# A hybrid decoder step on one core: where small loads, the convolution, the output weights and one projected block stand in the order

## The reference

```
h = RMSNorm(x);  p = h @ w_in                      # 1024 -> 2816 columns
group A (8 heads x 64): token shift  xs = p + (p_prev - p) * mu, LoRA decay, rate and gate,
    generalized delta-rule scan over tokens, GroupNorm per head, bonus, gate
group B (512 channels): u = value * sigmoid(gate); causal depthwise convolution, width 31;
    LayerNorm per token; z = z * sigmoid(z)
x = x + concat(yA, yB) @ w_out                     # group B is the lower half of w_out's rows
x = x + MoE(RMSNorm(x))                            # top 4 of 32 experts, clamped SwiGLU, d_ff 1024
y = RMSNorm(x)
```

## Time and profile before

| what | value |
|---|---|
| device time, median of 3 runs | 1236.3 us (1232.82 to 1236.37) |
| the profiled execution | 1236.51 us, its span 1234.7 us |
| mean granted TensorE clock | 0.993 of full speed |
| TensorE busy | 1192.9 us (97%), 8039 matmul records |
| VectorE busy | 452.5 us (37%) |
| ScalarE busy | 194.5 us (16%) |
| GpSimd busy | 73.5 us (6%) |
| read from HBM | 424.93 MB, mean 348 GB/s with the writes |
| instruction blocks fetched (queue q8) | 43 packets, 0.70 MB |

### The profile page before, as it was taken

How to read it: one execution, slowest core, us unless ns; L and a number is a source line. 1 busy time by engine, 2 the same in 40 slices (tenths; PEclk the granted TensorE clock), 3 DMA queues, 4 the chain that set the end, 5 groups by cost and what they waited for, 6 DMA issues and landing times.

```text
span 1234.7 us, 19155 instructions
## 1 busy us (share of the span) xinstructions
PE 1192.9 (97%) x8039; PEld 541.2 (44%) x8039; DVE 452.5 (37%) x987; ACT 194.5 (16%) x387; POOL 73.5 (6%) x113
## 2 busy tenths in 40 slices
PE   7999998999999999999999999999999999999995
PEld 5667798854333333333333333333333333333332
DVE  6657754243522333322222223323222222222324
ACT  3362223224100001100100000011000010000102
POOL 0303443030000000000000000000000000000000
PEclk9999999999999999999999999999999999999998
DMA  9521003288999999999999999999999999999994
GB/s 267 168 69 47 10 12 131 83 302 299 412 424 427 427 429 427 429 427 429 428 428 428 429 428 428 429 428 430 427 430 428 428 428 428 428 429 428 428 428 156
DMA packets 54637, 430.26 MB, mean 348 GB/s; under 512 B 13215, under 2 KB 26959, under 8 KB 29742
## 3 DMA queue, kind: packets, MB, share of 16 engines
q1 hardware_dynamic: 53146, 429.30, 84.1%
q10 hardware_dynamic: 1436, 0.16, 0.1%
HBM read 424.93 MB, written 4.48 MB: 348 GB/s over the span
## 4 chain that ended last, share of the span: by engine, by line
PE 66%; DMA 19%; DVE 2%; issue 0%; POOL 0%; ACT 0%; DVEq 0%
PE bank L1802 40%; DMA ring<-in_w_up_dram 19%; PE bank L1780 6%; PE bank L1856 5%; PE bank L1787 2%; PE bank L1027 2%; PE bank L1112 2%; PE bank L1670 2%; PE bank L1731 1%; PE bank L1810 1%; PE bank L983 1%; PE bank L1008 1%; PE bank L1828 1%; PE bank L1165 0%; PE bank L1161 0%
## 5 line engine op out<-in xcount | busy, mean ns | idle before, releaser
L1802 PE MATMUL bank<-ring,arena 128*64 128x512 f32 x1536 | 342.2, 594 | 7.2 <-DMA ring<-in_w_up_dram 6.5
L1802 PE MATMUL bank<-arena 128*64 128x512 f32 x1536 | 342.6, 593 | 6.5 <-DMA arena<-in_w_up_dram 6.5
L1802 PEld LDWEIGHTS bank<-ring,arena 128*64 128x64 f32 x1536 | 109.2, 137 | 218.5 <-issue 200.5
L1802 PEld LDWEIGHTS bank<-arena 128*64 128x64 f32 x1536 | 108.9, 136 | 217.5 <-issue 199.4
L2074 DVE TENSOR_SCALAR arena<-bank 128x512 f32<-128x512 f32 x32 | 22.1, 692 | 380.4 <-PE bank L1810 380.4
L2088 DVE TENSOR_TENSOR arena<-arena,bank 128x512 f32<-128x512 f32 x186 | 113.7, 679 | 1.6 <-PE bank L1856 1.6
L524 PE MATMUL bank<-arena,ring 128*128 128x336 f32 x352 | 104.0, 453 | 1.2 <-DVE arena L660 1.2
L1856 PE MATMUL bank<-arena 64*128 64x512 f32 (+1 forms) x384 | 91.1, 606 | 0.7 <-issue 0.7
L1780 PE MATMUL bank<-arena 128*64 128x512 f32 (+1 forms) x384 | 89.5, 600 | 0.1
L2078 DVE TENSOR_SCALAR arena<-bank 128x512 f32<-128x512 f32 x32 | 22.1, 691 | 176.6 <-PE bank L1810 176.6
L524 PEld LDWEIGHTS bank<-arena,ring 128*128 128x128 f32 x352 | 67.3, 193 | 35.0 <-issue 3.5
(11 more groups left out here) (356 smaller groups left out, 824.2 us busy)
## 6 DMA issues: line engine op xcount, KB each, us to landing
ring<-in_w_gate_dram SPq DMA_DIRECT2D x32, 2048.0 KB, 24.8
arena<-in_w_up_dram SPq DMA_DIRECT2D x32, 2048.0 KB, 27.9
ring<-in_w_down_dram SPq DMA_DIRECT2D x32, 2048.0 KB, 31.3
arena<-in_w_gate_dram SPq DMA_DIRECT2D x32, 2048.0 KB, 26.5
ring<-in_w_up_dram SPq DMA_DIRECT2D x32, 2048.0 KB, 29.0
arena<-in_w_down_dram SPq DMA_DIRECT2D x31, 2048.0 KB, 30.9
ring<-in_w_in_dram SPq DMA_DIRECT2D x11, 1024.0 KB, 5.3
ring<-in_w_out_dram SPq DMA_DIRECT2D x4, 1024.0 KB, 9.2
```

The lines of the kernel that those rows point to most:

```text
L1802: mm = M.matmul(bank[64 * hb:64 * hb + 64, b, :], tokens(cc), w[:, c, 512 * hb:512 * hb + 512], start=(cc == 0), stop=(w3 == 2 and cc == K ...
```

## The change

- **Start.** The second tile of x (128 rows) is loaded from ScalarE's queue instead of SyncE's, and ScalarE also takes its sum of squares; VectorE keeps the other two. One VectorE operation, 384 wide, makes the three diagonal tiles. The three products with ones go to PSUM bank 7, side by side, VectorE reads them there for `hT`, and the ScalarE copies and the buffer `rbc` are gone. `keep(7)` comes first among ScalarE's copies of x, since bank 7 has to be free. Six, four and three products of ones with ones (`idle_product`), whose result nobody reads, stand at the start of TensorE's list, ahead of the products with 1/rms, and behind them.
- **Vector loads.** Six of ScalarE's vector loads and the convolution weights and shift state move behind its copies of x. `project(1)` stands ahead of the transposes that use them.
- **Order of columns.** `IN_ORDER` takes the second half of the convolution's columns (units 8 and 10) ahead of the keys (2 and 3). `lay_out(2)` and `lay_out(3)` move up with them. TensorE's small products keep their order but stand behind other projections: `project(12)` ahead of `cumulate(2)`, three projections ahead of the key squares' sums, and all projections ahead of the bonus sums. ScalarE takes the exponentials ahead of the key squares.
- **Convolution.** All 124 steps are in stage one; `CONV_LATE`, `conv_late` and the waits for it in stage two are gone. VectorE runs 69 steps in a row after the second shift.
- **Output weights.** Each of the four `w_out` units is issued at a milestone of its own of the scan (`sk_done` 2, `n_done` 2, `e_ready` 3, `e_ready` 9).
- **Gates of z.** ScalarE's first sigmoid stands before the chunk loop, the other three in its first three passes; VectorE multiplies each in the same pass.
- **Projected blocks.** `project_z(0)` stands in the last pass of the chunk loop, ahead of its products; the third stage has blocks 1 to 7, in PSUM banks exchanged by one, and what stood after block d now stands after block d + 1. The four products and four additions that finish y are interleaved, and TensorE's first block of y waits for them one by one.

```diff
-CONV_LATE = 11
...
-IN_ORDER = [7, 9, 6, 2, 3, 8, 10, 0, 1, 4, 5]
+IN_ORDER = [7, 9, 6, 8, 10, 2, 3, 0, 1, 4, 5]
...
-rbc = take(NT)
...
-        sp.dma_start(xt[:, 1, :], a["x_prompt"][0, P - META:2 * P - META, :]).then_inc(x_in[1], 16)
...
+        act.dma_start(xt[:, 1, :], a["x_prompt"][0, P - META:2 * P - META, :]).then_inc(x_in[1], 16)
...
+        def load_vectors(first, last):
+            for k in range(first, last):
+                name, n = vectors[k]
...
+                act.dma_start(vrow[at:at + n, 0, :], src.rearrange("(c p) -> c p", p=P))\
+                    .then_inc(R["rows_in"], 16)
+
+        load_vectors(0, 7)
+        act.wait_ge(R["small_set"], 1)
+        act.wait_ge(x_in[1], 16)
+        A.activation(junk[1], xt[:, 1, :], ACT.Square, accum_out=small[:, 9:10]).then_inc(R["sq_ready"], 1)
+        act.wait_ge(R["ms_ready"], 1)
+        A.activation(small[:, 4:7], small[:, 0:3], ACT.Sqrt).then_inc(R["rms_ready"], 1)
+
+        def keep(c):
+            A.copy(xkeep[c], bank[:, c, 0:NT]).then_inc(R["xkeep_ready"], 1)
+
+        act.wait_ge(R["x_turned"], 3)
+        keep(KC - 1)
+        for c in range(KC - 1):
+            if c == 6:
+                act.wait_ge(R["idle_done"], 1)
+            keep(c)
+        load_vectors(7, len(vectors))
         act.dma_start(vrow[0:CW * 4, 1, :],
                       a["dw_weight"][0].rearrange("t (c p) -> (t c) p", p=P)).then_inc(R["rows_in"], 16)
         act.dma_start(vrow[0:NSEQ * NBA, 2, :],
                       a["state_shift"][0].rearrange("s (c p) -> (s c) p", p=P)).then_inc(R["rows_in"], 16)
-        act.wait_ge(R["ms_ready"], 1)
-        A.activation(small[:, 4:7], small[:, 0:3], ACT.Sqrt).then_inc(R["rms_ready"], 1)
-
-        def keep(c):
-            A.copy(xkeep[c], bank[:, c, 0:NT]).then_inc(R["xkeep_ready"], 1)
-
...
+        evacuate(6)
...
-        evacuate(6)
         evacuate(7)
...
         evacuate(8)
+        lay_out(2)
         for j in range(4):
...
         evacuate(9)
+        lay_out(3)
         for j in range(4):
...
         evacuate(10)
+        act.wait_ge(R["xkeep_stored"], 32)
+
+        def exps(j):
+            act.wait_ge(R["cum_done"], j + 1)
+            lx, li = bank[:, 4 + 2 * (j % 2), 0:NT], bank[:, 5 + 2 * (j % 2), 0:NT]
+            A.activation(eLx[:, j, :], lx, ACT.Exp)
+            A.activation(emL[:, j, :], li, ACT.Exp, scale=-1.0)
+            A.activation(eL[:, j, :], li, ACT.Exp).then_inc(R["exp_ready"], 1)
+
+        exps(0)
+        exps(1)
+        evacuate(11)
+        exps(2)
+        exps(3)
+        evacuate(12)
+        evacuate(13)
         act.wait_ge(R["shifted"], k_last)
         for j in range(4):
             A.activation(sqT[:, j, :], kT[:, j, :], ACT.Square, scale=vecA[:, V_KK + j:V_KK + j + 1])
...
-
...
-        evacuate(12)
-        lay_out(2)
-        evacuate(13)
-        lay_out(3)
+        evacuate(14)
...
-        evacuate(14)
+        evacuate(15)
...
-        for n in range(15, 20):
+        for n in range(16, 22):
             evacuate(n)
...
-        evacuate(20)
-        evacuate(21)
...
+        def idle_product(n):
+
+            for _ in range(n):
+                mm = M.matmul(bank[:, 6, 384:512], ones, ones, start=True, stop=True)
+            return mm
+
+        idle_product(6)
         for i, (t0, n) in enumerate(TILES):
             pe.wait_ge(x_in[i], 32 if i != 1 else 16)
             for c in range(KC):
                 mm = M.transpose(bank[:, c, t0:t0 + n], xt[0:n, i, P * c:P * c + P], ident[0:n, 0:n])
             mm.then_inc(R["x_turned"], 1)
+        idle_product(4)
         pe.wait_ge(R["rdiag_ready"], 1)
+        pe.wait_ge(R["xkeep_ready"], 1)
         for i, (t0, n) in enumerate(TILES):
-            M.matmul(bank[:, 5 + i, 384:384 + n], ones[0:n, :], rdiag[0:n, i, 0:n], start=True, stop=True)\
-                .then_inc(R["rbc_done"], 1)
+            mm = M.matmul(bank[:, 7, t0:t0 + n], ones[0:n, :], rdiag[0:n, i, 0:n], start=True, stop=True)
+        mm.then_inc(R["rbc_done"], 1)
+        pe.wait_ge(R["xkeep_ready"], 2)
+        idle_product(3).then_inc(R["idle_done"], 1)
...
-                pe.wait_ge(R["xkeep_ready"], n + 1)
+                pe.wait_ge(R["xkeep_ready"], n + 2)
...
         project(0)
+        project(1)
         pe.wait_ge(R["rows_in"], 16 * 15)
...
-        for n in range(1, 8):
+        for n in range(2, 8):
...
         project(11)
+        project(12)
         pe.wait_ge(R["exp_ready"], 1)
         cumulate(2)
         pe.wait_ge(R["exp_ready"], 2)
         cumulate(3)
-        project(12)
-        project(13)
+        for n in range(13, 16):
+            project(n)
         pe.wait_ge(R["exp_ready"], 3)
         pe.wait_ge(R["kk_sq"], 4)
...
-        project(15)
+        project(16)
+        project(17)
         pe.wait_ge(R["knx_ready"], 1)
...
-        for n in range(16, 20):
+        for n in range(18, 22):
             project(n)
...
-        project(20)
-        project(21)
...
-            dve.wait_ge(x_in[i], 32 if i != 1 else 16)
+            if i == 1:
+                continue
+            dve.wait_ge(x_in[i], 32)
             last = V.tensor_tensor_reduce(out=junk[i][0:n, :], in0=xt[0:n, i, :], in1=xt[0:n, i, :], scale=1.0,
...
+        dve.wait_ge(R["sq_ready"], 1)
...
-        for i in range(3):
-            last = V.tensor_scalar(rdiag[:, i, :], ident, small[:, 12 + i:13 + i], None, ALU.mult)
-        last.then_inc(R["rdiag_ready"], 1)
+        V.tensor_tensor(rdiag, b2(ident, 3), b3(small[:, 12:15], P), ALU.mult).then_inc(R["rdiag_ready"], 1)
         dve.wait_ge(R["g_in"], 16)
-        dve.wait_ge(R["x_turned"], 3)
-        dve.wait_ge(R["rbc_ready"], 3)
+        dve.wait_ge(R["rbc_done"], 1)
         for c in range(KC):
-            dve.wait_ge(R["xkeep_ready"], c + 1)
-            V.scalar_tensor_tensor(hT[:, c, :], xkeep[c], gcol[:, c:c + 1], rbc, ALU.mult, ALU.mult)\
-                .then_inc(R["hT_ready"], 1)
+            dve.wait_ge(R["xkeep_ready"], c + 2 if c < KC - 1 else 1)
+            V.scalar_tensor_tensor(hT[:, c, :], bank[:, 7, 0:NT], gcol[:, c:c + 1], xkeep[c],
+                                   ALU.mult, ALU.mult).then_inc(R["hT_ready"], 1)

...
-        for i, n in enumerate((6, 7, 7, 7, 7, 7)):
-            convolve(n)
+        convolve(6)
+        shift(0)
+        convolve(7)
+        shift(1)
+        convolve(69)
+        for i in range(2, 6):
             shift(i)
-        convolve(21)
+            convolve(10 if i < 5 else 6)
         dve.wait_ge(R["kk_sq"], 4)
         dve.wait_ge(R["ktmp_ready"], 4)
         dve.wait_ge(R["shifted"], 6)
         link(V.tensor_tensor(kT, kT, ktmp, ALU.mult))
-        dve.wait_ge(R["exp_ready"], 4)
-        link(V.tensor_tensor(kT, kT, emL, ALU.mult))
-        convolve(2)
         dve.wait_ge(R["kk_root"], 1)
         link(V.tensor_scalar(knorm, knorm, 1e-12, None, ALU.max))
         V.reciprocal(knorm, knorm).then_inc(R["kk_inv"], 1)
-        convolve(8)
+        dve.wait_ge(R["exp_ready"], 4)
+        link(V.tensor_tensor(kT, kT, emL, ALU.mult))
         shift(6)
-        convolve(6)
+        convolve(2)
         shift(7)
...
-        shift(8)
         link(V.tensor_tensor(bT, bT, emL, ALU.mult))
-        convolve(3)
+        convolve(2)
         shift(9)
...
-        for i, n in enumerate((5, 8, 8, 8)):
-            convolve(n)
-            shift(10 + i)
-        convolve(4 * CW - CONV_LATE - 113)
+        for i in range(10, 14):
+            shift(i)
...
-    sp.wait_ge(S["conv_step"], CONV_LATE)
-    for t in range(UNITS_IN, UPRE):
+    for t, (s, n) in zip(range(UNITS_IN, UPRE), (("sk_done", 2), ("n_done", 2), ("e_ready", 3), ("e_ready", 9))):
+        sp.wait_ge(S[s], n)
         load_unit(sp, t)
...
-    pool.wait_ge(S["conv_step"], CONV_LATE)
...
+
+    def z_gate(j):
+        act.wait_ge(S["z_affine"], j + 1)
+        nc.scalar.activation(zsg[:, j, :], zT[:, j, :], ACT.Sigmoid).then_inc(S["z_sig"], 1)
+
+    z_gate(0)
...
-        if c < 4:
-            act.wait_ge(S["z_affine"], c + 1)
-            nc.scalar.activation(zsg[:, c, :], zT[:, c, :], ACT.Sigmoid).then_inc(S["z_sig"], 1)
+        if c < 3:
+            z_gate(c + 1)
...
+        else:
+            project_z(pe, 0)
...
-        for _ in range((0, 6, 5, 0)[l]):
-            next(conv)
...
-        if c:
-            dve.wait_ge(S["z_sig"], c)
-            V.tensor_tensor(zT[:, c - 1, :], zT[:, c - 1, :], zsg[:, c - 1, :], ALU.mult)\
+        if c < 4:
+            dve.wait_ge(S["z_sig"], c + 1)
+            V.tensor_tensor(zT[:, c, :], zT[:, c, :], zsg[:, c, :], ALU.mult)\
                 .then_inc(S["zT_ready"], 1)
...
+def project_z(pe, d):
+
+    if d == 0:
+        pe.wait_ge(S["zT_ready"], 4)
+        wait_unit(pe, UNITS_IN)
+        wait_unit(pe, UNITS_IN + 1)
+    if d >= 2:
+        pe.wait_ge(F["zp_ready"], d - 1)
+    for cc in range(4, 8):
+        mm = nc.tensor.matmul(bank[:, (d + 1) % 2, 0:NT], out_rows(cc)[:, P * d:P * d + P], zT[:, cc - 4, :],
```

(25 more changed lines are left out.)

102 lines of the change are left out of this document (30 added, 72 removed).

## The result

The changed kernel takes 1242.4 us (median of 9 runs, 1236.7 to 1245.9) against 1236.4 for the kernel before in the same comparison: ratio 1.0042, 95% interval 1.0026 to 1.0057. It is slower by about 6 us, where 11 us less was forecast. The profiled execution took 1245.88 us with a span of 1244.1, 9.4 more than the one of before; among the 9 runs it is the slowest, so its sum is 3 us too large for the median.

The account below looks back on a forecast made before the run. TensorE was taken as the bound up to the experts, then the full DMA weight stream. Terms summed to -11.1 us, taking 1236.5 to 1225.4, say 1225.5, with a range of 1221.5 to 1233.

Parts of the forecast that it names:

- The stream: Experts: weight loads run without a hole from the ninth, so time saved earlier passes one for one; 11 us.
- first rival: Stage one: GpSimd's product waits 9 us during VectorE's 69 steps, gate products 6 late; price 7; 22% with milder cases.
- the race: Stage one: TensorE's key sums against VectorE's sixth shift and ScalarE's key squares; +0.5 us, bounds 0 and +4.5.
- Rows of x: Start: x on two queues and quicker 1/rms rows bring the first projection earlier; -1.8 us, bounds -0.5 and -4.
- shorter path: Start: VectorE reads the 1/rms products from PSUM itself, 1.4 us in place of 2.76; -1.35 us.
- Idle products: Start: they keep TensorE working, so its clock rises before the first projection; -2.2 us, at worst 0.
- Late vectors: Start: small vector loads moved behind the copies of x may land late; +0.5 us, bounds 0 and +4.
- Order of columns: Stage one: TensorE's wait of 1.82 us for exponentials goes, -1.8 us; the race comes in its place.
- Hole: Stage two: TensorE's 2.29 us hole after four loads issued at once goes when they are spaced; -2.3, at worst 0.
- Clock: Low-clock stretches go: behind the stage-two hole, -1.6 us, and at the z block in the last chunk, -3.0 us.
- Gate ahead of the loop: Before the chunk loop: a table load and pass on ScalarE precede the first negated U; +0.5 us, at worst +1.8.
- Less cover: After the chunk loop: each later step has one projected block less ahead of it; +0.7 us, bounds 0 and +2.3.

Follow-up runs that it names:

- e11_mended: Changed kernel with x on SyncE's queue, two small loads earlier, two VectorE pauses, eleven steps fewer before sixth shift, first z gate behind first U: 1230.7 us.
- e1_pause: Changed kernel with two pauses in VectorE's run of 69 steps, waiting for GpSimd's third and fourth products: 1238.6 us.
- e3_one_queue: Changed kernel with the second tile of x back on SyncE's queue: 1240.4 us.
- e7: Kernel before with the changed start, idle products included, and x all on SyncE's queue: 1233.2 us.
- e10: Kernel before with the changed start and x all on SyncE's queue, but without the idle products: 1237.0 us.
- e5_spaced_alone: Kernel before with one edit, the last three output weight units issued behind separate level steps instead of at once: 1236.5 us.
- e6_block_alone: Kernel before with first projected block in the last chunk pass, first gate ahead of the loop, gates multiplied in the same pass, last mean rows singly: 1236.7 us.
- e12_gate_ahead: e11_mended with the first gate of z ahead of the chunk loop, as in the change: 1231.3 us.
- e9_gate_behind: Changed kernel with the first gate of z back behind the first negated U: 1240.7 us.

## Why the prediction was wrong

**The stream.** Right: 9.3 us at the ninth load, 9.4 in the span, and -3.7 and -4.1 for the mended version.

**The step that failed** is the choice between the forecast and the first rival, "shut out". The sum took VectorE's run at 0.476 us a step with 2.6 us in all for sharing with GpSimd, and put GpSimd's delay at nothing, with the median of 14 subtractions as evidence. In its place the product took 10.14 us, and TensorE lost 6.0 us waiting and 3.1 at the lower clock. The rival's mechanism, place and wait came out as written (gate products 6 us late; measured 6.01), and its price was 7; the pauses of e1_pause gave 3.8 back in the medians, and the race behind them took 3.3. What misled me was a median of another operation. The instructions of the product's own line in the kernel before:

```profile
L318 POOL TENSOR_TENSOR arena<-arena x4: 892/896/897, 31.7 to 96.5; 128x336 f32<-128x336 f32 x4
```

All four ran while VectorE did nothing, so no row had the product beside convolution steps. Of the 14 subtractions ten met steps, and nine of these were over in 0.64 to 1.5 us, beside runs of 3 to 8 steps; the tenth, 4.67, ended 0.5 us after its run of eight. That row, and not the median, was the one like the new code. Why GpSimd gets in at some places and at others not, these runs leave open. It isn't the 69 steps alone: in the changed kernel two subtractions later on took 3.39 and 2.50 us beside runs of 18 and 10 steps, and each ended 0.5 us after its run. The Trainium skill (SBUF — State Buffer, SBUF: two separate sides) says that a VectorE instruction with two SBUF inputs and a GpSimd instruction that reads SBUF exclude each other, and that whoever comes first has the ports for the whole instruction. By it GpSimd would wait for one step. The trace agrees that one keeps the other out and differs in the length: back to back, 20 steps pass (10.14 us); with a short gap between steps, none (0.94).

**Rows of x.** Predicted -1.8, with bounds -0.5 and -4; measured +0.63 at the first projection. The step "the second queue could bring rows earlier" looked at the tile that came earlier and not at the one that shares the engines with it. On one queue the first projection is at 13.51 in e3_one_queue, -0.35, but at up to 14.95 in other profiles. Of the 1.35 for the shorter path, 1.04 are seen there (1.72 us from the products with ones to the first projection, before 2.76), but these products start 0.69 later than at 11.10, behind ScalarE's second table load, which I had not counted.

**Idle products.** -2.2; the first two projections take 2.2 less than before, and 1.7 less than without these products (e7 and e10). Right, and the time shows 3.8 in the medians.

**Late vectors.** +0.5; the wait is 0.91. Right within bounds.

**Order of columns.** The wait of 1.82 for exponentials is gone, as forecast. The race, +0.5 with a bound of +4.5, measured 3.3 in e1_pause and nothing with eleven steps fewer ahead of the shift. The bound does not come out of its own terms: 99 steps at 0.53 give 70.7 against 67.6, so +3.1, and the measured wait lies just above it. (In the same way, all bounds at their good ends give 1221 only with the early rows of x in it, and 1223 without.)

**Hole.** -2.3 against -1.9 in the changed kernel's chain: right there, and by luck. The cause as I put it, a queue four loads deep, fell with e5_spaced_alone. The mean product's wait went from 1.0 to 0.7 us, -0.3 against -0.4.

**Clock.** -1.6 behind the hole and -3.0 for the block: both failed. I took two low stretches of one profile for properties of the code. In the changed kernel's profile low stretches begin at 72.9, 113.8, 154.8, 209.4 and 257.2: the first z block is spared and the second is not. Two other kernels had neither of the old stretches with the code there unchanged (e6_block_alone behind the hole, e5_spaced_alone at the last chunk). Behind the barrier the lower level took 6.8 us in the changed kernel's profile and 5.1 before, so in place of -4.6 stands +1.7. Over all runs the clock costs the changed kernel 12.2 us and the one before 9.9; these 2.3 are nearly half of the 5.2 between the means. A part of them has a cause, the low stretch of 6.8 us that begins in the wait of 6 us.

**Gate ahead of the loop.** +0.5, at worst +1.8; TensorE waits 0.45 in the changed kernel, in e6_block_alone and in e12_gate_ahead. Right, cover included. The 2.04 on the chain misled me afterwards, in the forecasts for e9_gate_behind, e11_mended and e12_gate_ahead.

**Less cover.** +0.7; a wait of 0.20 in e6_block_alone and in the changed kernel. Small, as said.

**Together.** Between the forecast and the profiled execution lie 20.5 us. By the rows the wait and its low stretch are 9.1 of them, the two clock terms 6.3, the rows of x 2.4, the low stretch at 113.8 1.7, and the rest cancels; some 19 are found. The shut-out product is the largest; with its 9.1 alone the forecast of 1225.4 would have been 1234.5, outside the range by itself (an estimate from these rows).
